# A hybrid attention layer: another order of the steps in the attention loop, one copy on another engine, and other places for side work and weight loads

## The reference

```python
h = rmsnorm(x, norm_gain) * (1 + scale) + shift          # scale, shift, gate from c @ w_ada + b_ada
u_a, z_a, q, k, v, z_b, q_idx, k_idx, w_idx, g_a, g_b = split(h @ w_in)
y_a = multiscale_pool(u_a, w_pool_group, pool_scale) * silu(z_a)
q, k = rope(rmsnorm(q)), rope(rmsnorm(k))                # 8 heads of 64, one shared key/value head
score = sum_h relu(q_idx_h @ k_idx) * w_idx_h            # causal; the 256 best keys of each query
attn = softmax(q @ k / 8 over the selected keys) @ v
y_b = attn * silu(z_b)
merged = sigmoid(g_a) * (y_a @ w_branch_a) + sigmoid(g_b) * (y_b @ w_branch_b)
out = x + gate * (merged @ w_out)
```

## Time and profile before

| | busy us | share of the span |
|---|---|---|
| TensorE, matmuls | 806.9 | 94% |
| VectorE | 572.4 | 67% |
| GpSimd | 380.2 | 44% |
| ScalarE | 350.7 | 41% |

### The profile page before, as it was taken

One profiled execution on the slowest core, in us unless ns is written; L12 is line 12 of the kernel. 1 busy time (PEld: TensorE's weight loads), 2 busy tenths in 40 slices (PEclk: granted clock), 3 DMA queues, 4 the chain that ended last, 5 costly groups with the idle time before them and its releaser, 6 DMA issues.

```text
span 859.8 us, 13939 instructions
## 1 busy us (share of the span) xinstructions
PE 806.9 (94%) x4974; PEld 707.5 (82%) x4978; DVE 572.4 (67%) x1193; ACT 350.7 (41%) x647; POOL 380.2 (44%) x333
## 2 busy tenths in 40 slices
PE   3899999999999999999999998999898889999998
PEld 3699998889988888887788876777777767889998
DVE  5845538978888889888888156455657774663332
ACT  6473455664222222233422124767667762330000
POOL 1024534344425658934552107456877511792100
PEclk9899999999999999999999999999999999999999
DMA  9930110014422322220132225432422003744332
GB/s 355 356 99 2 50 50 26 13 36 124 135 62 74 98 74 73 88 84 20 30 121 97 87 101 193 150 123 79 149 81 75 24 18 130 244 141 143 111 99 74
DMA packets 62685, 87.95 MB, mean 102 GB/s; under 512 B 5881, under 2 KB 44317, under 8 KB 61726
## 3 DMA queue, kind: packets, MB, share of 16 engines
q1 hardware_dynamic: 48606, 64.04, 23.8%
q10 hardware_dynamic: 12096, 16.78, 5.4%
q0 software_dynamic: 1920, 6.29, 1.9%
HBM read 66.12 MB, written 20.97 MB: 101 GB/s over the span
## 4 chain that ended last, share of the span: by engine, by line
PE 82%; ACT 6%; DVE 4%; issue 3%; DMA 2%; SPq 1%; POOL 0%; DVEq 0%; ACTq 0%
PE pp L654 22%; PE pp L656 21%; PE pp L655 21%; PE pp L965 4%; PE pt L947 3%; PE ps L791 3%; PE ps L792 3%; DMA ada_w<-in_w_ada 2%; ACT prob L1332 2%; ACT pT L1324 1%; DVE pT L1903 1%; DVE prob L1962 1%; SPq L465 1%; PE pt L976 1%; DVE y_row L1915 1%
## 5 line engine op out<-in xcount | busy, mean ns | idle before, releaser
L597 POOL TENSOR_TENSOR w_lo<-w_raw,w_hi 128x1024 fp32r<-128x1024 f32 x50 | 123.4, 2486 | 216.5 <-ACT w_hi L592 165.0
L1840 DVE TENSOR_SCALAR_CACHE_REDUCE junk<-score,cand 128x384 uint8<-128x384 f32 (+1 forms) x186 | 168.6, 944 | 19.3 <-issue 13.3
L654 PE MATMUL pp<-hT_hi,w_hi 128*128 128x512 f32 x384 | 150.2, 391 | 0.0
L656 PE MATMUL pp<-hT_hi,w_lo 128*128 128x512 f32 x384 | 149.5, 389 | 0.0
L655 PE MATMUL pp<-hT_lo,w_hi 128*128 128x512 f32 x384 | 149.4, 389 | 0.0
L654 PE MATMUL pp<-w_hi,hT_hi 128*128 128x256 f32 x352 | 101.2, 287 | 0.5 <-ACT zb_out L1141 0.5
L656 PE MATMUL pp<-w_hi,hT_lo 128*128 128x256 f32 x352 | 99.4, 282 | 0.0
L655 PE MATMUL pp<-w_lo,hT_hi 128*128 128x256 f32 x352 | 99.4, 282 | 0.0
L1903 DVE TENSOR_TENSOR pT<-pt,pT 128x512 fp32r<-128x512 f32 (+3 forms) x96 | 50.9, 554 | 61.3 <-ACT pT L1324 60.6
L654 PEld LDWEIGHTS pp<-hT_hi,w_hi 128*128 128x128 f32 x384 | 72.1, 188 | 16.1 <-issue 0.8
L656 PEld LDWEIGHTS pp<-hT_hi,w_lo 128*128 128x128 f32 x384 | 72.1, 188 | 15.2
(11 more groups left out here) (269 smaller groups left out, 1828.0 us busy)
## 6 DMA issues: line engine op xcount, KB each, us to landing
w_raw<-in_w_in SPq DMA_DIRECT2D x36, 512.0 KB, 3.7
ada_w<-in_w_ada SPq DMA_DIRECT2D x7, 1024.0 KB, 11.6
sgb_spill<-stage ACTq DMA_DIRECT2D x16, 256.0 KB, 2.0
sga_spill<-stage ACTq DMA_DIRECT2D x16, 256.0 KB, 2.0
stage<-sga_spill SPq DMA_DIRECT2D x16, 256.0 KB, 3.0
ma_spill<-stage POOLq DMA_DIRECT2D x16, 256.0 KB, 2.4
gate_w<-in_w_ada SPq DMA_DIRECT2D x16, 256.0 KB, 2.7
w_raw<-in_w_out SPq DMA_DIRECT2D x8, 512.0 KB, 4.3
```

The lines of the kernel that those rows point to most:

```text
L597: nc.gpsimd.tensor_tensor(lo, raw, hi.bitcast(F32), ALU.subtract).then_inc(w_lo_done, 1)
L654: nc.tensor.matmul(o, a_hi, b_hi, start=first, stop=False)
L656: return nc.tensor.matmul(o, a_lo, b_hi, start=False, stop=last)
L1840: v.tensor_scalar(junk[:, n % 2, 0:keys(b)], score[:, score_at(b):score_at(b + 1)], least, None, ALU.is_ge, ALU.add, accum_out=cnt[:, n:n ...
```

## The change

On TensorE the logits of head i go ahead of the transposes of head i - 2. On ScalarE the exponential of head i - 1 goes ahead of the copy of head i - 2's transposes. On VectorE mask and maximum of head i go ahead of `outputs` and of `pT_low`, and VectorE takes over the copy of pv's result from ScalarE (`output_parts`). The 16 gate parts on GpSimd start at step 1 and come every third step, where they started at step 28 and came every second; the gate rows on TensorE go from steps 65 and 67 to 27 and 51. In SyncE's branch B loop the weight pieces go ahead of the loads for a merge, two pieces more are loaded in it after unit 15 and so ahead of the first rows of x, and the last piece goes ahead of the rows of x of tile 12.

```diff
-    GATE_AT = {2 * n + 28: n for n in range(16)}
-    GATE_ROWS = {65: 0, 67: 1}
+    GATE_AT = {3 * n + 1: n for n in range(16)}
+    GATE_ROWS = {27: 0, 51: 1}
...
             for n in range(16):
-                if n + 4 < 16:
-                    load_e(n + 4)
-                if n in WB_LAST and n < 15:
+                if n in WB_LAST:
                     for _ in range(1 if WB_LAST[n] < 2 else 2):
                         load_piece(nxt)
                         nxt += 1
+                if n + 4 < 16:
+                    load_e(n + 4)
             sp.wait_ge(m_raw_done, 16)
             for n in range(4):
                 load_x_row(n)
             for n in range(4 * NT - 4):
-                if n == 4:
-                    load_piece(nxt)
-                    load_piece(nxt + 1)
-                if n == NT + 4:
-                    for m in range(nxt + 2, len(pieces)):
+                if n == NT:
+                    for m in range(nxt, len(pieces)):
                         load_piece(m)
                 load_x_row(n + 4)
...
             for i in range(HEADS + 6):                    # TensorE
+                if i < HEADS:
+                    b, h = i // H, i % H
+                    if h == 0:
+                        pe.wait_ge(pt_free_a, pt_done[pt_at[("qT", b, 1)]][0])
+                    o = ps_claim(("S", i))
+                    two_pass(o, qT[:, b % 2, h, :], kT, keys(b)).then_inc(ps_full, 1)
                 if 0 <= i - 2 < HEADS:
                     ...                                   # transposes of head i - 2
-                if i < HEADS:
-                    ...                                   # the same lines as above
...
-                    pe.wait_ge(pp_free_a, pp_done[pp_at[("pv", 2 * n + 1)]][0])
+                    pe.wait_ge(pp_free_v, pp_done[pp_at[("pv", 2 * n + 1)]][1])
...
             for i in range(HEADS + 6):                    # ScalarE
+                if 0 <= i - 1 < HEADS:
+                    ...                                   # exponential of head i - 1
                 if 0 <= i - 2 < HEADS:
                     ...                                   # copy of head i - 2's transposes
-                if 0 <= i - 1 < HEADS:
-                    ...                                   # exponential of head i - 1
-                if 0 <= i - 5 < HEADS and i % 2 == 1:
-                    output_parts((i - 5) // 2)
...
+            def output_parts(u):                          # VectorE
+
+                dve.wait_ge(pv_done, u + 1)
+                if u >= 2:
+                    dve.wait_ge(pt_full, pt_at[("out", u // 2 - 1)] + 1)
+                v.tensor_copy(oT[:, u % 2, :, :].rearrange("p h q -> p (h q)"), pp[0][:, 0:2 * P]).then_inc(pp_free_v, 1)
...
             for i in range(HEADS + 6):
-                if 0 <= i - 5 < HEADS and (i - 5) % 4 == 3:
-                    outputs((i - 5) // 4)
-                if 0 <= i - 2 < HEADS:
-                    pT_low(i - 2)
+                if 0 <= i - 5 < HEADS and i % 2 == 1:
+                    output_parts((i - 5) // 2)
                 if i < HEADS:
                     ...                                   # mask and maximum of head i
+                if 0 <= i - 5 < HEADS and (i - 5) % 4 == 3:
+                    outputs((i - 5) // 4)
+                if 0 <= i - 2 < HEADS:
+                    pT_low(i - 2)
```

More of the change, by code:

```diff
@@ L144, in hybrid_layer @@
     pp_bank = [n % 2 for n in range(PP_HT)]
-    pp_uses += [("wa", n // 4, n % 4) for n in range(WA_FIRST)]
-    pp_bank += [n % 2 for n in range(WA_FIRST)]
+    pp_uses += [("wa", i, u) for i in range(4) for u in range(4)]
+    pp_bank += [n % 2 if n < WA_FIRST else 1 for n in range(16)]
     HEADS = NT * H
-    GATE_AT = {2 * n + 28: n for n in range(16)}
-    GATE_ROWS = {65: 0, 67: 1}
+    GATE_AT = {3 * n + 1: n for n in range(16)}
+    GATE_ROWS = {27: 0, 51: 1}
     for i in range(HEADS + 6):
-        if 0 <= i - 5 < HEADS and i % 2 == 1:
-            pp_uses.append(("pv", (i - 5) // 2))
+        if 0 <= i - 4 < HEADS and i % 2 == 0:
+            pp_uses.append(("pv", (i - 4) // 2))
             pp_bank.append(0)
-        if i in WA_STEP:
-            pp_uses.append(("wa", WA_STEP[i] // 4, WA_STEP[i] % 4))
-            pp_bank.append(1)
         if YB_STEP.get(i, NT - 1) < NT - 1:
@@ L169, in hybrid_layer @@
         last_in[pp_bank[n]] = n
-        by_act = n < PP_HT or use[0] in ("wa", "yb", "pv")
+        by_act = n < PP_HT or use[0] in ("wa", "yb")
         by_dve = not by_act or use[0] == "yb"
@@ L1297, in q_copies @@
                                          ACT.Copy).then_inc(pt_free_a, 1)
[L1299 to L1305, removed]
             def gate_copy(g):
@@ L1316, in _ @@
             for i in range(HEADS + 6):
+                if 0 <= i - 1 < HEADS:
+                    j, b, h = i - 1, (i - 1) // H, (i - 1) % H
+                    act.wait_ge(logit_done, j + 1)
+                    if h % 4 == 0 and b >= 2:
+                        act.wait_ge(o_sum, 2 * (b - 1))
+                    r = (b % 2) * H + h
+                    nc.scalar.activation(prob[:, j % 3, 0:keys(b)], prob[:, j % 3, 0:keys(b)], ACT.Exp, scale=-1.0,
+                                         bias=neg_max[:, j % 2:j % 2 + 1],
+                                         accum_out=row_sum[:, r:r + 1]).then_inc(prob_done, 1)
                 if 0 <= i - 2 < HEADS:
```

## The result

| | us, median | against the kernel before |
|---|---|---|
| before, same chip | 862.63 (861.74 to 863.68, 4 runs) | 1 |
| after | 893.59 (three of 4 runs: 893.50 to 893.66) | 1.0358 (95%: 1.0338 to 1.0379) |

The fourth run of after took 4452.51 us; it is left out of the ratio, and the median without it is 893.52. The change costs 31.0 us. Slower was forecast, but by 4.9 us, and 893.6 is far outside the range of 859 to 873. The profiled execution of after took 895.17 us (span 893.1), 33.4 over that of before.

What follows compares the result with a forecast made beforehand. TensorE, busy for 94% of the span, was taken as the bound. 861.74 - 2.2 (loop and tail) + 5.7 (stall for the rows of x) + 1.4 (clock behind it) = 866.6 us; range 859 to 873.

Steps and rivals of the forecast that it cites:

- Part 1: Attention loop, new order: waits of 17.1 and 13.1 us go; from step 28 on it gains 6.4 us.
- step 36 to 52: Attention loop: 45.5 us of work, four stalls of about 1.85 and 0.5 for latencies, 53.4 against 55.0.
- what is late next: Attention loop: `outputs` behind the mask frees `pt` late, a 1.8 us stall after each of 8 out transposes.
- it costs nothing: Attention loop below block 4: `outputs` behind the mask costs 0, since the `pt` buffer is needed a step later.
- VectorE's own load is last: Attention loop, steps 52 to 63: VectorE's work of some 3.4 us per step sets 37.8 us, against 40.1.
- Part 2: Gate parts on GpSimd: TensorE stands 7 us at step 20, 6.1 behind; clock adds 1.4, tail gains 3.2.
- no bound: GpSimd's queue: loads of gate weights have over 6 us each and so hold nothing up.
- 8 steps of room: GpSimd's queue: its other waiters, copies of branch A's units and `outputs`, have this much slack.
- Part 3: Output projection: rows of x land late behind weight pieces; TensorE stalls 5.7 us, clock adds 1.4.
- GpSimd isn't last at step 20: Rival, attention loop: GpSimd's intervals shrink, the loop gains 10.6 us, time 858.2; chance 0.13.
- rows in time: Rival, output projection: rows of x come without a stall, time 859.5 us; chance 0.05.
- VectorE holds the whole loop: Rival, attention loop: some 13 us more VectorE work, steps from block 4 on cost 5 us, time 871.6; chance 0.23.

Runs made afterwards that it cites:

- order_only: Kernel before with only the new order of the attention loop and the copy on VectorE; gate places and loads as before: 870.63 us, ratio 1.0105.
- outputs_before_mask: order_only with `outputs` alone put ahead of the mask on VectorE, `pT_low` still behind it: 855.24 us, ratio 0.9922 to the kernel before.
- both_scores_first: Kernel before with copy on VectorE, logits first on TensorE in all steps, new ScalarE and VectorE order only below step 32: 853.55 us, ratio 0.9906.
- copy_first_scores_first: copy_first with the logits ahead of the transposes on TensorE; ScalarE and VectorE keep the old order: 856.64 us, ratio 0.9930 to the kernel before.
- both_gate_rows: both_scores_first with the gate rows in steps 47 and 61 instead of 65 and 67: 853.00 us, ratio 0.9890 to the kernel before.
- copy_first: Kernel before with ScalarE's `output_parts` moved to the head of its step: 860.96 us, ratio 0.9996.
- order_gate: Kernel after with the loads as before, so new order and gate places together: 886.83 us, ratio 1.0290 to the kernel before.
- order_parts_rows_late: order_gate with the gate rows at steps 65 and 67 instead of 27 and 51: 885.55 us, ratio 1.0272 to the kernel before.
- gate_only: Kernel before with only the new places of gate parts and gate rows: 872.82 us, ratio 1.0119.
- load_only: Kernel before with only SyncE's new order of loads: 867.42 us, ratio 1.0069.
- order_mask_last: order_only with VectorE's mask behind `outputs` and `pT_low` again: 878.30 us, ratio 1.0195 to the kernel before.

## Why the prediction was wrong

**Part 1, the term that failed.** The prediction took 17.1 + 13.1 us of waits as gone, put one new wait in (`outputs` behind the mask, 8 times 1.8 us = 14.4), and gave "step 36 to 52" as "45.5 of work and four stalls of about 1.85" with 0.5 for latencies, 53.4. Here are its stretches beside what the profiles show, in us from query transposes to query transposes, the last to the mask of step 63:

| steps | forecast | before | after | order_only | outputs_before_mask | both_scores_first |
|---|---|---|---|---|---|---|
| 20 to 28 | 19.3 | 19.4 | 22.7 | 17.2 | 17.0 | 17.3 |
| 28 to 36 | 21.2 | 23.8 | 22.6 | 22.7 | 21.0 | 21.7 |
| 36 to 52 | 53.4 | 55.0 | 64.9 | 60.4 | 53.0 | 53.6 |
| 52 to 63 | 37.8 | 40.2 | 45.4 | 45.5 | 42.4 | 40.8 |

(The forecast and after have a gate row in steps 20 to 28; 1.4 us for the clock there were forecast beside the 19.3.)

The stall that it named is right in mechanism and in size. In the list of after it has 14.7 us; from step 36 to 52 it makes 60.4 - 53.0 = 7.4, which is four times 1.85; and putting that call alone back gives 15.4 and 14.9 us. This is the piece in the kernel after, at step 52: mask, sum, and the transposes behind them.

```profile
682.29 1.09 DVE L1951 CUSTOM_DVE_ANT_0 prob<-ps,bias 128x896 f32<-128x896 f32 x1 [3.17 <-PE ps L786]
...
683.63 0.66 DVE L1906 TENSOR_REDUCE y_row<-pt 128x256 f32<-128x512 f32 x1
...
684.49 1.72 PE L947 MATMUL pt<-ident,prob 128*128 128x128 f32 x7 [2.24 <-DVEq L1910]
```

What failed is the rest of that sum, the 46.0 of work and latencies in which TensorE waits for nothing else. (The pieces of work that the prediction names come to 42.8 for these steps, 43.8 with a gate row, so its 45.5 holds some 2 us that it doesn't name.) With the stalls for `outputs` gone these steps still take 53.0, so 7.0 more, and the list of outputs_before_mask has 6.6 us of waits for `pT_low` in them. The prediction didn't ask for it under "what is late next", though `pT_low` frees `pt` buffers too. Four transposes of an out group (L970) take the buffer that the first group of head i - 2 used in the same step, and wait for `pT_low`, which waits for the mask of head i:

```profile
678.80 0.63 PE L970 MATMUL pt<-ident,oT 128*128 128x128 f32 x4 [2.16 <-DVE pT L1887]
```

In the whole loop these waits and those of the probability transposes behind them are 10.9 + 4.8 = 15.7 us. That the mask stands ahead of `pT_low` makes only a part of them. With `pT_low` ahead of the mask and the logits first on TensorE the out transposes still wait 8.4 us for it (copy_first_scores_first) or 8.1 (both_gate_rows), against 2.8 with TensorE's old order (copy_first). And what the old order on ScalarE and VectorE saves here it gives to the wait for the exponential, 0.7 in outputs_before_mask and 4.8 in both_gate_rows; both_scores_first is no quicker from step 36 to 52 (53.6). So both orders have about the same waits left, under other names. How much of them another order could take away isn't shown.

In the kernel after, steps 36 to 52 take 4.5 us more than in order_only, which is what the row of step 51 costs in order_gate (see order_parts_rows_late). The prediction had a wait behind the row of step 27 and none behind this one.

The second error is of kind. A wait in the list was taken as time to be had. The list of the earlier trace rows is that of the weight loads; the matmuls' own waits of the same two names are 10.7 + 5.8 = 16.5 us, not 30.2. And copy_first took the largest one away and the time stayed (ratio 0.9996), because TensorE then waited for the next thing on the same buffers. With the stall for `outputs` gone, where the prediction's numbers give a gain of some 6.4 + 14.4 = 21, the order gains 6.8.

**Below block 4 "it costs nothing".** Right: order_only gains 3.5 us to step 21, its steps 21 to 29 take 17.2 us where before has 19.8, and with `outputs` ahead of the mask they take 17.1.

**Steps 52 to 63, "VectorE's own load is last".** Wrong: 37.8 us forecast, 45.5 in order_only and 45.4 in after (from the query transposes of step 52 to the mask of step 63: 689.00 to 734.38). VectorE isn't full there: it is busy for 30.7 of the 45.4 us, and TensorE's waits for `outputs` and `pT_low` go on. Even with `outputs` ahead of the mask these steps take 42.4. The forecast had no clock term here, but from 660 to 700 the granted clock is 0.92 in order_only and 0.91 in outputs_before_mask, where before has 1.00.

**Part 2, GpSimd.** The mechanism is right: GpSimd in order, the query transposes of step 20 the instruction that waits. The forecast had GpSimd's third `q_stk` end at 573.3; it ended at 578.72. The rows of GpSimd in the kernel after say where the difference is:

```profile
536.94 1.56 POOL L1532 TENSOR_SCALAR gate_acc<-gate_w,c_silu 128x512 f32<-128x512 f32 x1 [0.87 <-DMA gate_w<-in_w_ada]
...
548.09 1.29 POOL L1520 TENSOR_TENSOR stage<-a_out,stage 128x512 f32<-128x512 f32 x1 [2.46 <-ACT a_out L1270]
...
564.25 0.73 POOL L1564 TENSOR_TENSOR y_row<-y_row,z_row 128x256 f32<-128x256 f32 x1 [1.73 <-DVE y_row L1906]
...
577.46 1.26 POOL L1510 TENSOR_TENSOR q_stk<-q_row,q_stk 128x512 fp32r<-128x512 f32 x1
...
578.82 1.23 PE L888 MATMUL pt<-ident_r,q_stk 128*128 128x128 f32 x8 [7.62 <-POOL q_stk L1510]
```

The sum of its intervals was 37.3 us; from 536.1 to 578.7 are 42.6, and three waits of 0.87 + 2.46 + 1.73 = 5.1 make up nearly all of the difference. The first is for the first load of gate weights, which the prediction took for "no bound". It also missed a stall at step 4: the first gate part stands ahead of that block's query rest too, so TensorE waits 2.7 us there. The second wait is for the copy of TensorE's next unit of branch A, the third for VectorE's `outputs`, to which it gave "8 steps of room". That the stall at step 4 brought the second is argued from their order in time. A queue that was forecast "without a gap" had gaps. So TensorE's transposes of step 20 were 11.5 late (578.82 against 567.27), not 6.1, and the difference of 5.4 is GpSimd's (578.7 against 573.3).

Of the clock behind the stall, 1.4 was forecast. gate_only's steps 21 to 29 take 22.4 against 19.8: 1.0 for the gate row, 1.6 left. The tail was forecast at -3.2 and gave -4.6 in gate_only's profile.

**Part 3, SyncE.** Right in mechanism and near in size: 7.1 forecast (5.7 of stall, 1.4 of clock), 5.5 alone and 6.2 in the whole; the stall measured 4.9 in load_only and 5.1 in after. The merge loads were put at 0 to 1: VectorE waits 1.6 and 2.7 us for one of them, and no wait of TensorE in the list comes from it. The rows of after that answer to the earlier trace rows:

```profile
790.83 5.23 POOL L591 TENSOR_TENSOR w_lo<-w_raw,w_hi 128x1024 fp32r<-128x1024 f32 x2
...
793.28 3.19 SPq L454 DMA_DIRECT2D w_raw<-in_w_out  x2
...
796.51 13.97 SPq L513 DMA_DIRECT2D x_row<-in_x  x8
800.33 0.42 DVE L1980 TENSOR_TENSOR o_row<-pp,gate 128x256 f32<-128x256 f32 x1 [6.53 <-DMA x_row<-in_x]
800.81 0.58 PE L648 MATMUL pp<-w_hi,mT_hi 128*128 128x256 f32 x1 [5.09 <-DVE o_row L1980]
```

The rows of x leave SyncE right behind the two pieces (793.28 + 3.19 = 796.47), and the first ones land 3.7 us later (3.5 in load_only). The Trainium skill, DMA: Bandwidth & Descriptors, section "Anatomy of one DMA — SWDGE (gpsimd) path", says that a wait on a semaphore happens on the issuing sequencer before dispatch. By that rule the rows can't go past the waiting piece, and this trace agrees: they leave at 796.51, behind it.

**The rivals.** "GpSimd isn't last at step 20" is refuted by the rows above, "rows in time" by load_only. "VectorE holds the whole loop" has the right engine and the wrong reason: what counts is where its instructions stand, since the same load with one call moved (outputs_before_mask) is 15.4 us faster.

**What stays open.** The surplus of order and gate places is 5.2 in medians and 9.0 in single profiles with `outputs` behind the mask, 4.5 and 4.7 with it ahead. In the profiles some 6 of the 9.0 stand in the two stretches with a gate row (2.2 in steps 20 to 28, 3.9 in 44 to 52), but moving the rows late lowered the median by 1.3 only. The waits for `pT_low` were not taken away by themselves: with `pT_low` ahead of the mask and ScalarE's new order the ring of order_mask_last appears, with ScalarE's old order other waits take their place.

## What to carry to other kernels

When steps are put in another order on one engine, list for every buffer who frees it, and look where each of these now stands; one found isn't all. A wait that disappears is worth only what the next one on the same buffer leaves of it, so ask for the sum, or try the edit alone, before counting it. Work moved to an idle engine costs where another engine waits for something behind it in its queue, and its queue can be late by more than its own work (42.6 us where 37.3 were counted), since it waits for others as well.

## What the runs showed that was not expected

What a gap costs behind itself isn't the same from kernel to kernel. In the projection of the kernel after, TensorE stands 5.09 us and then runs 24 matmuls, one tile, at a granted clock of 0.50 (the 1.2 GHz level), from the table by stretches:

```profile
800.00:806.00 6.00, 5.19 (x24) 0.50 0.37 123
806.00:812.00 6.00, 6.00 (x52) 0.99 0.27 81
```

From its first matmul to VectorE's read of the result this tile takes 5.51 us (800.81 to 806.32). In the kernel before, the first tile takes 3.21 at full clock (764.04 to 767.25), so 2.3 us are the clock's. In load_only, behind a gap of 4.86 us, the tile takes 4.62 (773.52 to 778.14), 1.4 of it the clock's, as forecast. Gaps of nearly one length had two prices.
